# Attention scores of a gated linear attention layer with exchanged operands: four column groups, a copy by ScalarE and a turn by TensorE

## The chip, the core and the metric

The kernel runs on one core of one Trainium2 chip, as one launch. The metric is the device time of the launch in microseconds (us). Before the change it is 1719.86 us, the median of 3 runs (1718.37 to 1725.63).

## The reference

A decoder trunk of two layers for a prompt (1024 tokens) and 8 short samples (8 tokens each), in f32. Layer 0 mixes tokens by causal pooling, layer 1 by gated linear attention (GLA) with four heads. Only the prompt's part of layer 1 is touched by the change. Cut to it, for each head, with chunks of 32 tokens (`b` is the running sum of the log decay within a chunk):

```
q_dec = q * exp(bcum);  k_intra = k * exp(-bcum);  k_state = k * exp(blast - bcum)
att = where(causal, q_dec @ k_intra.T, 0)
o = att @ v + q_dec @ s                      # s: the state before the chunk
s = exp(blast) * s + k_state.T @ v
```

Then `o` is normed, gated by silu(z) and projected. The products are f32.

## The kernel before

Everything is written in Bass with explicit semaphores: each engine has its own list of instructions, and waits stand where the author put them. Nothing is reordered by a scheduler. TensorE is called PE in the rows, VectorE DVE, ScalarE ACT, GpSimd POOL.

The prompt is worked in 8 super-chunks of 128 tokens (`SUP = 4 * CH`, `NSUP = 8`), four chunks of 32 in each. With a decay that is summed over all 128 tokens, `Kp[:, b, :]` holds the 128 keys as chunk `b` of the queries sees them, and `qd` the 128 queries. In each head a loop over steps `s = 0..9` runs on three engines at once:

- **PE** (lines 1865 to 1887): `fill(1)`, then `scores(s+1)` (L1756, into the PSUM bank X[0]), `key_rows(s+1)` (L1766, a transpose by identity), `output(s)` (L1774: scores times values; L1782: queries times state, from s = 1), `update(s)` (L1791: the state's update, into ps[1][:, 2]), `fill(FILL_STEP - 1)`, which is one more fill, `mean_square` (L1846), on even steps from 2 `sample_inter` (L1811: the samples' queries times their state, in column groups of 32), and from step 2 `sample_update` (L1823, L1824), which overwrites ps[1][:, 2] and so waits for `S_ready` of the same step. A `fill` is one eighth of a gate projection Z0, Z1 or Z2: nine passes on L515 into psA. It has nothing to do with the recurrence and is put between its parts. Eight fills make a projection; the next one may start only when ACT has read psA out (`gate_in`, L1140, a Silu).
- **ACT** (lines 1148 to 1165): in step s `gate_in` if s is 0 or 4, `ksT_out(s+1)` (L1117), `exps(s+2)` (L1098 four times into Kp, L1102, L1105), `o_out(s)` (L1129, L1130), `exp_qs(s+1)` (L1111). Silu and Exp need different tables of ACT, so each `gate_in` has an ACT_TABLE_LOAD before it and the next `exps` has one too.
- **DVE** (lines 1472 to 1485): `ks_rows(s-2)`, `att_out(s+1)` (L1398: copies the scores under the causal mask to SBUF), `qd_args(s+2)` (L1376, L1377), `scale_qk(s+2)` (L1385, L1387), `state(s)` (L1406, L1410), `scale_qs(s+1)` (L1391), `sample_state(s-2)` (L1424).
- **POOL** multiplies Kp by the keys (L881) after each `exps`, then sums squares (L890, L892).

A semaphore count is per super-chunk: `att_done` is raised by `scores`, `att_ready` by `att_out`, `kp_ready` by POOL, `evac` by `gate_in`. `wait_apart` is a wait against a register's value.

Of the kernel before, what the change touches and what calls it, by code (L numbers as in the profile page):

```python
# [24 lines left out]
P = 128  # L25
# [5 lines left out]
KG = GW // P  # L31
# [10 lines left out]
CH = 32  # L42
SUP = 4 * CH
NSUP = TP // SUP
# [46 lines left out]
def trunk(nc, x_prompt, x_sample, c_prompt, c_sample, state_pool, state_gla, ada_w, ada_b, norm_g,  # L91
# [4 lines left out]
    ACT, ALU = mybir.ActivationFunctionType, mybir.AluOpType  # L96
# [3 lines left out]
    with ctx:  # L100
# [128 lines left out]
        def sem(name):  # L229
            return ctx.enter_context(nc.semaphore(name))  # L230
# [43 lines left out]
        kp_zero, kp_exp, kp_ready = sem("kp_zero"), sem("kp_exp"), sem("kp_ready")  # L274
        qd_arg, qd_exp, qd_ready = sem("qd_arg"), sem("qd_exp"), sem("qd_ready")
        qs_exp, qs_ready, ks_exp, ks_ready = sem("qs_exp"), sem("qs_ready"), sem("ks_exp"), sem("ks_ready")
        att_done, att_ready, o_done, o_evac = sem("att_done"), sem("att_ready"), sem("o_done"), sem("o_evac")
        kT_done, ksT_ready, upd_done, S_ready = sem("kT_done"), sem("ksT_ready"), sem("upd_done"), sem("S_ready")
        smp_arg, smp_exp, smp_ready = sem("smp_arg"), sem("smp_exp"), sem("smp_ready")
# [24 lines left out]
        def wait_apart(eng, what, count):  # L304


            count = eng.to_reg(count)
            eng.wait_ge(vec_ready, 1)
            eng.wait_ge(what, count)
# [606 lines left out]
        def _(act):  # L916
# [125 lines left out]
            def head(g, first):  # L1042
# [65 lines left out]
                def exp_qs(s):  # L1108
                    if s >= 1:
                        act.wait_ge(o_done, g * NSUP + s)  # L1110
                    nc.scalar.activation(qs[:], L[:, s * SUP:(s + 1) * SUP], ACT.Exp).then_inc(qs_exp, 1)  # L1111

                def ksT_out(s):
                    act.wait_ge(kT_done, g * NSUP + s + 1)
                    if s >= 2:
                        act.wait_ge(upd_done, g * NSUP + s - 1)
                    nc.scalar.activation(ksT[:, s % 2, :], ps[1][:, 1, 0:P], ACT.Copy).then_inc(ksT_ready, 1)  # L1117
# [31 lines left out]
                exp_qs(0)  # L1149
                act.wait_ge(smp_kT, g + 1)  # L1150
                nc.scalar.activation(ksT_s[:], ps[1][:, 1, 0:P], ACT.Copy).then_inc(smp_ksT, 1)
                ksT_out(0)
                exps(1)
                for s in range(NSUP):
                    if s in (0, 4):
                        gate_in(s // 4)
                    if s + 1 < NSUP:
                        ksT_out(s + 1)
                    if s + 2 < NSUP:
                        exps(s + 2)  # L1160
                    o_out(s)
                    if s + 1 < NSUP:
                        exp_qs(s + 1)
                    if s in (1, 5):
                        split_slot(L1, GP, act, g, GP.slot["Z2"] + s // 4)
# [44 lines left out]
        def _(dve):  # L1210
# [134 lines left out]
            with dve.Fori(0, NG) as g:  # L1345
# [25 lines left out]
                def qd_args(s):  # L1371

                    c0 = s * SUP
                    if s >= 1:
                        dve.wait_ge(att_done, g * NSUP + s)
                    nc.vector.tensor_copy(qd[:, 0:CH], L[:, c0:c0 + CH])  # L1376
                    nc.vector.tensor_tensor(qd[:, CH:SUP].rearrange("p (b t) -> p b t", b=3),  # L1377
                                            L[:, c0 + CH:c0 + SUP].rearrange("p (b t) -> p b t", b=3),
                                            L[:, c0 + CH - 1:c0 + SUP - 1:CH].unsqueeze(2).broadcast_to([P, 3, CH]),
                                            ALU.subtract).then_inc(qd_arg, 1)  # L1380
# [11 lines left out]

                def att_out(s):

                    if s >= 2:
                        wait_apart(dve, o_done, g * NSUP + s - 1)
                    wait_apart(dve, att_done, g * NSUP + s + 1)
                    nc.vector.copy_predicated(att[:, s % 2, :], causal[:], X[0][:, 0:P])\  # L1398
                        .then_inc(att_ready, 1)

                def state(s):
# [11 lines left out]
                def ks_rows(b):  # L1413

                    if b >= 1:
                        dve.wait_ge(smp_upd, g * NB + b)
                    link(nc.vector.tensor_scalar(ksm[:, 0, :], ksT_s[:], seq_rows[:, b:b + 1], None, ALU.mult))
                    nc.vector.scalar_tensor_tensor(out=ksm[:, 1, :], in0=ksT_s[:], scalar=seq_rows[:, b:b + 1],  # L1418
                                                   in1=ksm[:, 0, :].bitcast(f32), op0=ALU.mult,
                                                   op1=ALU.subtract).then_inc(ksm_ready, 1)  # L1420
# [51 lines left out]
                for s in range(NSUP + 2):  # L1472
                    if s >= 2:
                        ks_rows(s - 2)
                    if s + 1 < NSUP:
                        att_out(s + 1)
                    if s + 2 < NSUP:
                        qd_args(s + 2)
                        scale_qk(s + 2)
                    if s < NSUP:  # L1480
                        state(s)
                    if s + 1 < NSUP:
                        scale_qs(s + 1)
                    if s >= 2:
                        sample_state(s - 2)
# [43 lines left out]
        def _(pe):  # L1529
# [179 lines left out]
            def head(g, first):  # L1709
# [38 lines left out]
                def scores(s):  # L1748
                    pe.wait_ge(kp_ready, g * NSUP + s + 1)
                    pe.wait_ge(qd_ready, g * NSUP + s + 1)  # L1750
                    if s >= 1:
                        pe.wait_ge(att_ready, g * NSUP + s)
                    else:
                        pe.wait_ge(smp_attr, g + 1)
                    for b in range(4):
                        last = nc.tensor.matmul(X[0][:, b * CH:(b + 1) * CH], Kp[:, b, :], qd[:, b * CH:(b + 1) * CH],  # L1756
                                                start=True, stop=True)
                    last.then_inc(att_done, 1)

                def key_rows(s):  # L1760
                    pe.wait_ge(ks_ready, g * NSUP + s + 1)
                    if s >= 1:
                        pe.wait_ge(ksT_ready, g * NSUP + s)
                    else:
                        pe.wait_ge(smp_ksT, g + 1)
                    nc.tensor.transpose(ps[1][:, 1, 0:P], ks[:], ident[:]).then_inc(kT_done, 1)  # L1766

                def output(s):

                    pe.wait_ge(att_ready, g * NSUP + s + 1)  # L1770
                    if s >= 1:
                        pe.wait_ge(o_evac, g * NSUP + s)
                    for e in range(KG):
                        last = nc.tensor.matmul(ps[1][:, 0, e * P:(e + 1) * P], v[:, s, e * P:(e + 1) * P],  # L1774
                                                att[:, s % 2, :], start=(e == 0), stop=(s == 0 and e == KG - 1),
                                                skip_group_check=True)
                    if s:
                        pe.wait_ge(S_ready, g * NSUP + s)
                    pe.wait_ge(qs_ready, g * NSUP + s + 1)
                    if s:  # L1780
                        for e in range(KG):
                            last = nc.tensor.matmul(ps[1][:, 0, e * P:(e + 1) * P], S[:, e * P:(e + 1) * P],  # L1782
                                                    qs[:], start=False, stop=(e == KG - 1), skip_group_check=True)
                    last.then_inc(o_done, 1)

                def update(s):

                    pe.wait_ge(ksT_ready, g * NSUP + s + 1)
                    if s >= 3:
                        pe.wait_ge(s0_ready, g * NB + s - 2)  # L1790
                    nc.tensor.matmul(ps[1][:, 2, :], ksT[:, s % 2, :], v[:, s, :], start=True,  # L1791
                                     stop=True).then_inc(upd_done, 1)
# [72 lines left out]
                fill(1)  # L1865
                scores(0)
                key_rows(0)
                fill(FILL_START - 5)
                for s in range(NSUP + 2):
                    if s <= NSUP:  # L1870
                        fill(1)
                    if s + 1 < NSUP:
                        scores(s + 1)
                        key_rows(s + 1)
                    if s < NSUP:
                        output(s)
                        update(s)
                        fill(FILL_STEP - 1)
                    if 1 <= s <= NSUP:
                        pe.wait_ge(att_ready, g * NSUP + min(s + 2, NSUP))  # L1880
                        mean_square(s - 1)
                    if s in (2, 4, 6, 8):
                        sample_inter(s - 2)
                    if s == NSUP + 1:
                        sample_out()
                    if s >= 2:
                        sample_update(s - 2)
# [64 lines left out]
```

## Time and profile before

| what | value |
|---|---|
| median of 3 runs | 1719.86 us |
| the profiled execution | 1722.27 us |
| its span (first to last instruction) | 1720.5 us |
| granted TensorE clock, mean | 0.98 |
| PE busy / PEld (weight loads) busy | 96% / 91% |
| DVE, ACT, POOL busy | 48%, 28%, 23% |

The attention loops of the four heads start their first scores at about 895, 1117, 1340 and 1563 us of the span. Within a head the starts of the eight blocks of scores on L1756 lie 5.4, 5.7, 6.8, 8.3, 7.3, 8.3 and 7.3 us apart, the same in all four heads within 0.02 us.

Busy shares are averages over the whole span. In the steps of the attention PE is busy nearly without a gap, so the question for each edit is what PE has to do, and what it would have to wait for.

### The profile page before, as it was taken

What the parts mean: (1) busy time and instruction counts of PE and PEld (TensorE: products, weight loads), DVE (VectorE), ACT (ScalarE), POOL (GpSimd) and SP (SyncE); (2) the same over time, 40 slices, a digit from 0 to 9 for tenths busy, and PEclk for the clock granted to TensorE, in tenths of its full rate; (3) what the DMA queues carried; (4) which work ended last, traced back from release to release, by engine and by line L of the source; (5) the groups of instructions that cost most, each with busy time, mean ns of one, the idle gap of its engine ahead of it and who ended that gap; (6) DMA issues with size and microseconds to landing.
All of it is one profiled execution on the core that took longest, in us unless ns stands there. A gap on an engine that the chain in (4) does not pass through costs nothing.

```text
span 1720.5 us, 26408 instructions
## 1 busy us (share of the span) xinstructions
PE 1644.9 (96%) x10307; PEld 1564.1 (91%) x10307; DVE 833.3 (48%) x1245; ACT 483.5 (28%) x1021; POOL 397.3 (23%) x392
## 2 busy tenths in 40 slices
PE   6899999999999999997999999999999999999997
PEld 3798999999999999996898899988999889998896
DVE  4494439453844475456224561235621456324465
ACT  4321112110211111134335403264132532225423
POOL 3221212121221212113224121232112331213310
PEclk8999999999999999997999999999999999999999
DMA  9322211221222122210112211122111221111212
GB/s 352 129 62 72 75 44 55 74 76 39 67 76 62 53 66 71 67 27 26 37 38 75 80 39 50 37 62 80 51 38 37 62 92 38 41 47 38 98 43 104
DMA packets 145621, 115.23 MB, mean 67 GB/s; under 512 B 5885, under 2 KB 128345, under 8 KB 145506
## 3 DMA queue, kind: packets, MB, share of 16 engines
q1 hardware_dynamic: 143680, 112.87, 21.3%
q8 instruction: 91, 1.49, 0.4%
q10 hardware_dynamic: 1834, 0.74, 0.2%
q14 instruction: 16, 0.13, 0.0%
HBM read 99.05 MB, written 15.00 MB: 66 GB/s over the span
## 4 chain that ended last, share of the span: by engine, by line
PE 88%; DVE 8%; ACT 2%; issue 1%; DMA 1%; SPq 0%; POOL 0%; ACTq 0%; DVEq 0%
PE psA L515 45%; PE psB L515 29%; PE psB L1774 2%; PE psB L1791 2%; PE psX L1756 2%; DVE PQ L1273 2%; PE psB L1782 1%; PE psX L1811 1%; DMA ada<-in_ada_w 1%; PE psB L1823 1%; DVE y_rows L1523 1%; PE psX L1636 1%; DVE a_hi L591 1%; ACT PQ L1049 1%; DVE ksm L1418 1%
## 5 line engine op out<-in xcount | busy, mean ns | idle before, releaser
L322 POOL TENSOR_TENSOR w_lo<-stage,w_hi 128x1024 fp32r<-128x1024 f32 x112 | 279.0, 2492 | 1059.4 <-ACT w_hi L317 1059.4
L515 PE MATMUL psA<-h_hi,w_hi 128*128 128x362 f32 (+1 forms) x1152 | 277.4, 350 | 24.5 <-DVE h_lo L453 15.3
L515 PE MATMUL psA<-h_lo,w_hi 128*128 128x362 f32 (+1 forms) x1152 | 256.9, 332 | 0.0
L515 PE MATMUL psA<-h_hi,w_lo 128*128 128x362 f32 (+1 forms) x1152 | 255.6, 330 | 0.0
L515 PEld LDWEIGHTS psA<-h_hi,w_hi 128*128 128x128 f32 x1152 | 202.4, 192 | 53.5 <-issue 48.3
L317 ACT ACTIVATE w_hi<-stage 128x1024 fp32r<-128x1024 f32 x112 | 120.1, 1072 | 392.3 <-PE psB L515 301.3
L515 PEld LDWEIGHTS psA<-h_lo,w_hi 128*128 128x128 f32 x1152 | 204.2, 193 | 0.0
L515 PEld LDWEIGHTS psA<-h_hi,w_lo 128*128 128x128 f32 x1152 | 203.4, 192 | 0.0
L515 PE MATMUL psB<-h_hi,w_hi 128*128 128x362 f32 (+1 forms) x576 | 129.1, 332 | 1.7 <-ACT kT L1049 1.7
L515 PE MATMUL psB<-h_hi,w_lo 128*128 128x362 f32 (+1 forms) x576 | 126.3, 327 | 0.0
L515 PE MATMUL psB<-h_lo,w_hi 128*128 128x362 f32 (+1 forms) x576 | 126.2, 327 | 0.0
L515 PE MATMUL psA<-a_hi,w_hi 128*128 128x362 f32 (+1 forms) x480 | 108.2, 333 | 5.9 <-DVE a_lo L594 5.9
L515 PE MATMUL psB<-a_hi,w_hi 128*128 128x362 f32 (+1 forms) x480 | 106.0, 329 | 4.2 <-DVE a_lo L1294 4.2
L515 PE MATMUL psA<-a_lo,w_hi 128*128 128x362 f32 (+1 forms) x480 | 105.7, 328 | 0.0
L515 PE MATMUL psB<-a_hi,w_lo 128*128 128x362 f32 (+1 forms) x480 | 105.6, 328 | 0.0
L515 PE MATMUL psA<-a_hi,w_lo 128*128 128x362 f32 (+1 forms) x480 | 105.3, 327 | 0.0
L515 PE MATMUL psB<-a_lo,w_hi 128*128 128x362 f32 (+1 forms) x480 | 105.3, 327 | 0.0
L515 PEld LDWEIGHTS psB<-h_hi,w_hi 128*128 128x128 f32 x576 | 98.3, 189 | 7.4 <-issue 6.3
L1273 DVE SCALAR_TENSOR_TENSOR PQ<-PQ,win_on 128x1220 f32<-128x1220 f32 (+2 forms) x48 | 103.2, 2150 | 2.8 <-DVE PQ L1268 0.5
L515 PEld LDWEIGHTS psB<-h_hi,w_lo 128*128 128x128 f32 x576 | 99.9, 188 | 0.0
L515 PEld LDWEIGHTS psB<-h_lo,w_hi 128*128 128x128 f32 x576 | 99.8, 188 | 0.0
L1364 DVE COPY v<-psB 128x512 f32<-128x512 f32 x32 | 20.6, 686 | 150.2 <-PE psB L1719 150.2
(314 smaller groups left out, 2369.7 us busy)
## 6 DMA issues: line engine op xcount, KB each, us to landing
stage<-in_gla_w_in SPq DMA_DIRECT2D x40, 512.0 KB, 3.9
stage<-in_pool_w_in SPq DMA_DIRECT2D x32, 512.0 KB, 4.1
ada_stage<-in_ada_w SPq DMA_DIRECT2D x24, 512.0 KB, 3.5
ada<-in_ada_w SPq DMA_DIRECT2D x8, 1024.0 KB, 12.2
stage<-in_pool_w_out SPq DMA_DIRECT2D x16, 512.0 KB, 3.5
v<-in_state_gla SPq DMA_DIRECT2D x32, 256.0 KB, 2.6
out_new_gla_sample<-v SPq DMA_DIRECT2D x32, 256.0 KB, 2.1
stage<-in_gla_w_out SPq DMA_DIRECT2D x16, 512.0 KB, 3.6
```

Of the source, the lines that this page charges most:

```text
L317: nc.scalar.activation(w_hi[:, j % 2, :], stage[:, j % 2, :], ACT.Copy).then_inc(lay.hi_done, 1)
L322: nc.gpsimd.tensor_tensor(w_lo[:, j % 2, :], stage[:, j % 2, :], w_hi[:, j % 2, :].bitcast(f32), ALU.subtract).then_inc(lay.lo_done, 1)
L515: last = nc.tensor.matmul(ps[u][:, t, 0:width], weight(w[:, p, :], k), a[:, k, n0:n0 + width], start=(k == 0 and pas == 0), stop=(k == kt ...
L591: nc.vector.tensor_copy(a_hi[:, i, :], oT[:, i, :]).then_inc(chain_v, 1)
L1049: last = nc.scalar.activation(dst[:, n0:n0 + w], ps[GP.set[u]][:, t, 0:w], ACT.Copy, scale=scale)
L1273: link(nc.vector.scalar_tensor_tensor(out=dst[:, lo:WE], in0=src[:, lo - sh:WE - sh], scalar=win_on[:].rearrange("p g k -> p (g k)")[:, ds ...
L1364: nc.vector.tensor_copy(v[:, 4 * half:4 * half + 4, i * P:(i + 1) * P], ps[1][:, half, :].rearrange("p (s n) -> p s n", s=4))
L1418: nc.vector.scalar_tensor_tensor(out=ksm[:, 1, :], in0=ksT_s[:], scalar=seq_rows[:, b:b + 1], in1=ksm[:, 0, :].bitcast(f32), op0=ALU.mult, ...
L1523: nc.vector.scalar_tensor_tensor(out=y_rows[0:n, s, :], in0=ps_y[s % 3][0:n].rearrange("p a n -> p (a n)"), scalar=y_rms[0:n, s:s + 1], in ...
L1756: last = nc.tensor.matmul(X[0][:, b * CH:(b + 1) * CH], Kp[:, b, :], qd[:, b * CH:(b + 1) * CH], start=True, stop=True)
L1774: last = nc.tensor.matmul(ps[1][:, 0, e * P:(e + 1) * P], v[:, s, e * P:(e + 1) * P], att[:, s % 2, :], start=(e == 0), stop=(s == 0 and e ...
L1791: nc.tensor.matmul(ps[1][:, 2, :], ksT[:, s % 2, :], v[:, s, :], start=True, stop=True).then_inc(upd_done, 1)
```

## The change

`scores` exchanges its operands. Before, a chunk's 128x128 keys were the weights and its 32 queries moved past them, one chunk after the other, and the result stood as keys by queries. Now a chunk's 32 queries are the weights, in one of four column groups of 32, and its 128 keys move; the four results stand in four groups of partitions, as queries by keys. `output` needs keys by queries. So ACT copies the block from PSUM to SBUF (`scores_out`, into the second half of `att`), and PE turns it by identity (`turn_scores`) into the same place of PSUM from where DVE masks it. `att` has one buffer for the masked scores now in place of two. The rest is the order: `turn_scores(s+1)` stands behind `update(s)`, `scores_out(s+1)` first in ACT's step, and `qd_args` ahead of `att_out` on DVE.

```diff
+                def scores_out(s):
+                    act.wait_ge(att_done, g * NSUP + s + 1)
+                    if s >= 1:
+                        act.wait_ge(turn_done, g * NSUP + s)
+                    nc.scalar.activation(att[:, 1, :], X[0][:, 0:P], ACT.Copy).then_inc(score_out, 1)
...
                 exp_qs(0)
                 act.wait_ge(smp_kT, g + 1)
                 nc.scalar.activation(ksT_s[:], ps[1][:, 1, 0:P], ACT.Copy).then_inc(smp_ksT, 1)
+                scores_out(0)
                 ksT_out(0)
                 exps(1)
                 for s in range(NSUP):
+                    if s + 1 < NSUP:
+                        scores_out(s + 1)
                     if s in (0, 4):
                         gate_in(s // 4)
...
                 def att_out(s):
-                    if s >= 2:
-                        wait_apart(dve, o_done, g * NSUP + s - 1)
-                    wait_apart(dve, att_done, g * NSUP + s + 1)
-                    nc.vector.copy_predicated(att[:, s % 2, :], causal[:], X[0][:, 0:P])\
+                    if s >= 1:
+                        wait_apart(dve, o_done, g * NSUP + s)
+                    wait_apart(dve, turn_done, g * NSUP + s + 1)
+                    nc.vector.copy_predicated(att[:, 0, :], causal[:], X[0][:, 0:P])\
                         .then_inc(att_ready, 1)
...
+                    if s + 2 < NSUP:
+                        qd_args(s + 2)
                     if s + 1 < NSUP:
                         att_out(s + 1)
                     if s + 2 < NSUP:
-                        qd_args(s + 2)
                         scale_qk(s + 2)
...
-                        last = nc.tensor.matmul(X[0][:, b * CH:(b + 1) * CH], Kp[:, b, :], qd[:, b * CH:(b + 1) * CH],
+                        last = nc.tensor.matmul(X[0][b * CH:(b + 1) * CH, 0:P], qd[:, b * CH:(b + 1) * CH], Kp[:, b, :],
                                                 start=True, stop=True)
                     last.then_inc(att_done, 1)
+
+                def turn_scores(s):
+                    pe.wait_ge(score_out, g * NSUP + s + 1)
+                    nc.tensor.transpose(X[0][:, 0:P], att[:, 1, :], ident[:]).then_inc(turn_done, 1)
...
-                                                att[:, s % 2, :], start=(e == 0), stop=(s == 0 and e == KG - 1),
+                                                att[:, 0, :], start=(e == 0), stop=(s == 0 and e == KG - 1),
...
                 scores(0)
                 key_rows(0)
+                turn_scores(0)
                 fill(FILL_START - 5)
...
                     if s < NSUP:
                         output(s)
                         update(s)
+                    if s + 1 < NSUP:
+                        turn_scores(s + 1)
+                    if s < NSUP:
                         fill(FILL_STEP - 1)
```

ACT, from the end of `exps(1)` into step 0 of the first head, before (PQ<-psA is `gate_in`, ksT<-psB is `ksT_out`, Kp<-L is `exps`):

```order
L1102 ACTIVATE qd<-qd 128x128 [waits qd_arg]
L1105 ACTIVATE ks<-L 128x128 [waits kT_done]
L1140 ACT_TABLE_LOAD
L1140 ACTIVATE PQ<-psA 128x364 [waits gla_unit_done]
L1140 ACTIVATE PQ<-psA 128x362 x2
L1117 ACTIVATE ksT<-psB 128x128 [waits kT_done]
L1098 ACT_TABLE_LOAD
L1098 ACTIVATE Kp<-L 128x32 [waits att_done]
```

The same place after the change (all lines of ACT's part have moved by some numbers; att<-psX is `scores_out`):

```order
L1103 ACTIVATE qd<-qd 128x128 [waits qd_arg]
L1106 ACTIVATE ks<-L 128x128 [waits kT_done]
L1119 ACTIVATE att<-psX 128x128 [waits turn_done,att_done]
L1148 ACT_TABLE_LOAD
L1148 ACTIVATE PQ<-psA 128x364 [waits gla_unit_done]
L1148 ACTIVATE PQ<-psA 128x362 x2
L1125 ACTIVATE ksT<-psB 128x128 [waits kT_done]
L1099 ACT_TABLE_LOAD
L1099 ACTIVATE Kp<-L 128x32 [waits att_done]
```

The copy of the scores, with its wait for `att_done`, now stands between the last exponential and the load of the Silu table, which had no wait ahead of it.

DVE, in step 0 of the first head, before (att<-causal,psX is `att_out`, the writes of qd and ks are `scale_qk`, S<-psB is `state`):

```order
L1398 COPY_PREDICATED att<-causal,psX 128x128 [waits att_done,vec_ready]
L1376 COPY qd<-L 128x32 [waits att_done]
L1377 TENSOR_TENSOR qd<-L 128x96
L1384 REGISTER_ALU
L1385 TENSOR_TENSOR qd<-qd,qT 128x128 [waits qd_exp]
L1387 TENSOR_TENSOR ks<-ks,kT 128x128 [waits ks_exp]
L1404 ISA
L1406 COPY S<-psB 128x512 [waits upd_done,S_stored]
```

And after:

```order
L1388 TENSOR_TENSOR qd<-L 128x96
L1409 COPY_PREDICATED att<-causal,psX 128x128 [waits vec_ready,turn_done,o_done]
L1395 REGISTER_ALU
L1396 TENSOR_TENSOR qd<-qd,qT 128x128 [waits qd_exp]
L1398 TENSOR_TENSOR ks<-ks,kT 128x128 [waits ks_exp]
L1415 ISA
L1417 COPY S<-psB 128x512 [waits upd_done,S_stored]
```

`att_out` has moved behind the arguments of qd, and waits for the turn and for the output before it; both scalings and the state's update stand behind it.

## Rows read from the trace of the kernel before

**Rows 1.** The page: busy time and the chain that ended last.

```profile
PE 1644.9 (96%) x10307; PEld 1564.1 (91%) x10307; DVE 833.3 (48%) x1245; ACT 483.5 (28%) x1021; POOL 397.3 (23%) x392
...
PE 88%; DVE 8%; ACT 2%; issue 1%; DMA 1%; SPq 0%; POOL 0%; ACTq 0%; DVEq 0%
```

**Rows 2.** The chain in step 5 of head 0: start us, length us, what.

```profile
937.27 0.81 PE psX L1756 x8
938.08 0.14 PE psB L1766
938.22 0.89 PE psB L1774 x8
939.11 0.89 PE psB L1782 x8
940.01 0.86 PE psB L1791 x2
940.87 1.50 PE psA L515 x9
```

**Rows 3.** The chain around a product in column groups of layer 0.

```profile
155.80 0.57 PE psX L1636 x16
156.38 1.71 PE psB L515 x9
```

**Rows 4.** Timeline, head 0, before and in steps 0 and 1: start us, length us, what.

```profile
896.36 0.28 ACT L1117 ACTIVATE ksT<-psB 128x128 f32<-128x128 f32 x1 [2.36 <-PE psB L1766]
...
900.65 0.97 PE L1756 MATMUL psX<-qd,Kp 128*128 128x32 f32 x8
900.85 1.20 ACT L1140 ACTIVATE PQ<-psA 128x364 f32<-128x364 f32 x3 [1.50 <-PE psA L515]
...
903.53 1.03 ACT L1098 ACTIVATE Kp<-L 128x32 f32<-128x32 f32 x4
...
904.64 1.45 POOL L881 TENSOR_TENSOR Kp<-Kp,kT 128x32 f32<-128x32 f32 x4 [5.57 <-ACT Kp L1098]
...
906.33 0.97 PE L1756 MATMUL psX<-qd,Kp 128*128 128x32 f32 x8
```

**Rows 5.** Timeline, head 0, end of step 3 and step 4.

```profile
925.72 1.28 ACT L1140 ACT_TABLE_LOAD   x1
...
928.76 0.97 PE L1756 MATMUL psX<-qd,Kp 128*128 128x32 f32 x8
928.96 1.20 ACT L1140 ACTIVATE PQ<-psA 128x364 f32<-128x364 f32 x3 [1.96 <-PE psA L515]
...
932.90 0.29 DVE L1385 TENSOR_TENSOR qd<-qd,qT 128x128 f32<-128x128 f32 x1 [2.49 <-ACT qd L1102]
...
933.44 0.74 DVE L1410 SCALAR_TENSOR_TENSOR S<-S,dec,psB 128x512 f32<-128x512 f32 x1
...
935.04 0.19 PEld L1823 LDWEIGHTS psB<-v_s,ksm 128*128 128x128 f32 x1 [0.84 <-issue]
```

**Rows 6.** Timeline, head 0, step 5.

```profile
938.21 0.30 DVE L1398 COPY_PREDICATED att<-causal,psX 128x128 f32<-128x128 int8 x1 [1.07 <-PE psX L1756]
...
939.67 0.29 DVE L1385 TENSOR_TENSOR qd<-qd,qT 128x128 f32<-128x128 f32 x1 [0.92 <-ACT qd L1102]
...
939.97 0.33 DVE L1387 TENSOR_TENSOR ks<-ks,kT 128x128 f32<-128x128 f32 x1
...
940.91 0.75 DVE L1410 SCALAR_TENSOR_TENSOR S<-S,dec,psB 128x512 f32<-128x512 f32 x1 [0.61 <-PE psB L1791]
...
942.31 0.19 PEld L1823 LDWEIGHTS psB<-v_s,ksm 128*128 128x128 f32 x1
```

**Rows 7.** Busy us (instructions) of PE, PEld, DVE, ACT, POOL; granted clock; DMA.

```profile
960.70:964.10 3.40, 2.00 (x18) 1.81 (x16) 3.06 (x3) 2.54 (x5) 2.13 (x1) 1.00 0.29 106
964.13:967.54 3.41, 3.02 (x9) 2.83 (x10) 1.68 (x3) 0.56 (x1) 0.96 (x3) 0.50 0.01 5
...
199.50:202.90 3.40, 1.96 (x12) 1.96 (x13) 1.52 (x4) 0.00 (x0) 0.00 (x0) 1.00 0.45 154
```

More of the change, by code:

```diff
@@ L276, in trunk @@
         qs_exp, qs_ready, ks_exp, ks_ready = sem("qs_exp"), sem("qs_ready"), sem("ks_exp"), sem("ks_ready")
+        score_out, turn_done = sem("score_out"), sem("turn_done")
         att_done, att_ready, o_done, o_evac = sem("att_done"), sem("att_ready"), sem("o_done"), sem("o_evac")
```

## The prediction

> **What bounds the kernel now.** I read the page first. PE is busy for 96% of the span and makes up 88% of the chain that ended last [rows 1], so a change counts by what it adds to PE's own work or by what PE has to wait for. The granted clock is 0.98 on average. Next the chain inside one step of the attention [rows 2]: PE runs without a hole, and the step is a plain sum. The scores take 0.81 us for 8 passes (each f32 product is two), the transpose of the keys 0.14, the two halves of the output 0.89 each, the update 0.86, one fill of nine passes 1.50. Last the timeline of ACT, DVE and POOL beside it, to see how early each product of theirs is: the places where a delay would show are the two steps of a head with a Silu (steps 0 and 4), where ACT has no slack. There the Silu starts 0.20 us after the first scores, at 900.85 against 900.65 and at 928.96 against 928.76 [rows 4, 5], since it reads what PE's last fill has just left, and its table was loaded long before, at 925.72, while ACT waited [rows 5].
>
> **PE's own work.** The scores are 32 blocks (8 steps, 4 heads). No row shows a block of 4 products in column groups with 128 moving columns, but layer 0 has one with 8 products, 16 passes [rows 3]. It stands in the chain with 0.57 us, and the nine passes behind it take 1.71 where they take 1.50 elsewhere [rows 2, 3]: 0.21 us go into changing over. Passes of four groups run beside each other: a round of four takes about a quarter of the time of four in a row. Half of the 16 passes cost 0.22 less (two rounds of about 0.11), so our block costs 0.57 - 0.22 + 0.21 = 0.56 us, against 0.81. That is -0.25 a block. Bounds: at best the whole of 16 passes is halved, 0.28 + 0.21 = 0.49; at worst the eight passes run one after the other at the 0.11 of today's, plus the changeover, 1.1 us, so -0.32 to +0.3. I take -0.25, since the row is of the same form. The turn is one pass of the form of the keys' transpose, +0.14 [rows 2]. Both together are -0.1 us a step, -3.2 us in 32 blocks, if nothing waits.
>
> The Trainium skill (TensorEngine Tiling (Array Packing), "Theoretical Speedup") gives up to four times for a dimension of 32 or less. By that the blocks would go from 0.81 to 0.20 us, an estimate of -19.5 us in all, and -15 with the turns. The Trainium skill (TensorEngine Tiling (Array Packing), "Key Properties") also says that changing the tiling mode drains the engine, and the trace agrees with that one: 0.21 us behind such a block [rows 3]. By the drain most of the fourfold is given back.
>
> **The first block of a head.** Nothing but the keys' transpose stands between `scores(0)` and `turn_scores(0)`. ACT needs 0.28 us for its copy [rows 4] and about 0.15 for the two hand-overs. The scores have landed about 0.52 after their start (the 0.56, less what the changeover takes behind them), so the turn can't begin before 0.52 + 0.05 + 0.28 + 0.20 = 1.05 us and ends its pass at 1.19; before, the fill behind began at 0.81 + 0.14 = 0.95. So +0.24 us a head, where the cover of the other steps (output and update) is missing.
>
> **Step 0: the copy ahead of the Silu.** `scores_out(1)` waits for `att_done`, and it stands ahead of the table load in ACT's order. Until now the load was hidden in ACT's idle time. Now it follows: scores done at 900.65 + 0.52 = 901.17; hand-over 0.05, copy 0.28, a little to retire, load 1.28 [rows 4, 5], so the Silu starts at 902.82, not 900.85: ACT is 1.97 us late with everything queued behind it in the step. Who waits for that?
> - PE's next fill needs psA, which the Silu frees at 902.82 + 1.20 = 904.02. PE is there at 900.65 + 0.56 + 0.14 + 0.89 + 0.86 + 0.14 = 903.24 (step 0 has only one half of the output). It starts about 904.13: a wait of 0.9.
> - The next scores need Kp. Its exponentials move from 903.53 to 905.50, POOL's product from 904.64 to 906.61, ending at 908.06 in place of 906.09 [rows 4]. PE, after two fills, is there at 904.13 + 3.00 = 907.13: another 0.9.
> The second block of scores then starts at 908.05 and not at 906.33 [rows 4]: +1.72 us a head.
>
> **Step 4.** The same shift: scores done at 929.28, Silu at 930.94, not 928.96, +1.98. psA is free at 932.14, when PE just arrives (two halves of the output), and Kp is early. But on DVE the update of the state stands behind the scaling of qd and ks, which needs ACT's exponentials: qd moves from 932.90 to 934.88, the state from 933.44 to 935.42, ending at 936.16 [rows 5]. `sample_update` may not overwrite the update before that; its weights, loaded at 935.04 now, would be due at 934.94 and go in at about 936.2. +1.25, less 0.1 for PE's own work: +1.15 us a head.
>
> **Steps 3 and 5.** Here `sample_update` comes soon, there is no `sample_inter` before it. `att_out` now waits for the turn and takes scaling and state with it. With the scores started at 937.11, the turn begins 0.56 + 0.14 + 0.89 + 0.89 + 0.86 = 3.34 later, at 940.45, and lands about 0.3 later (its pass is short, its latency not); 0.13 hand-over, then copy 0.30, qd 0.29, ks 0.33, which overlap a little, and the state 0.75 [rows 6]: done about 942.45, against 941.66 now. The weights on L1823 would be due at 942.31 - 0.10 = 942.21 [rows 6]. A wait of 0.25 to 0.35, net +0.2 in each of the two. In steps 2 and 6 `sample_inter` covers it, in step 1 there is no such product: -0.1 each. The single `att` buffer costs nothing: the turn stands behind `o_done` of the output anyway, and the scores of the next step come a fill later. `qd_args` ahead of `att_out` keeps ACT's exponential of qd from waiting for the turn.
>
> Sum of a head: 0.24 + 1.72 + 1.15 + 2 x 0.2 - 3 x 0.1 = 3.2 us, 12.8 us in four heads.
>
> **The clock.** At the end of the first head PE is idle for 1.40 us between narrow products (busy 2.00 of 3.40), and then the granted clock is 0.50 for 3.41 us [rows 7], 1.2 GHz in place of 2.4, which costs half of that, 1.7 us. A stretch in layer 0 with as little (1.96 of 3.40), but with wide passes around it, is followed by full clock [rows 7]. The change adds two holes of 0.9 in steps 0 and 1 and one of 1.25 in step 4, this one behind the narrow `sample_inter`. None to all eight could bring such a drop, 0 to 13.6 us. I take two, +3.4: the hole of step 4 is the kind that did it, yet shorter.
>
> So the profiled execution would go from 1722.3 by 12.8 + 3.4 = 16 to about 1738; against the median of the runs, which is 2.4 below that execution, 1736 us.
>
> **Rivals.**
> - *No late Silu.* If ACT's Silu came in time in spite of the order (the table load running while ACT waits for `att_done`), the copy would cost it only 0.33 + 0.32 us, both waits of step 0 and the one of step 4 would shrink to nearly nothing, and the sum is the -3.2 of PE's work plus 1 to 3: 1717 to 1720, no change. For it: loads do stand ahead of waits today (925.72). Against it: after the change the load has the waiting copy ahead of it on an engine that works in order. It decides from the point where ACT's delay falls under about 0.8 us. 0.11.
> - *Faster.* The same, and the column groups give the fourfold with little changeover: -10 to -15, 1705 to 1711. Against it is the 0.21 of [rows 3]. 0.05.
> - *The column groups do not run beside each other* with 128 moving columns, +0.5 a block over my term: 16 us more, 1752. Against it [rows 3]. 0.03.
> - *The clock falls in every hole*: eight drops, 12.8 + 13.6: 1746. 0.17.
> - *The forecast*, with zero to four drops, 1731 to 1741. 0.64.
>
> The range holds the forecast, most of the clock's rival, and reaches towards the first: 1725 to 1748. About 0.5% (8.6 us) is what a measurement of this kernel can tell from no change: faster 0.05 (the fourfold), within it 0.13 (the first rival and a tail of 0.02 of the forecast), slower 0.82 (the rest).
>
> **What would show it.** In the profile after: blocks of scores with about 0.35 us in the chain and 1.7 for what follows; PE's waits named by ACT's Silu (psA) and POOL's Kp in step 0, by DVE's state ahead of `sample_update` in steps 3, 4, 5; the Silu 2.2 us behind the scores and not 0.2; starts of the scores 7.4 apart in step 0 in place of 5.7, and 9.5 in place of 8.3 in step 4. I am wrong if the load stands ahead of the copy in time, or if the head is not some 3 us longer.

## The result: 6.4 us slower, where 15 were forecast

| | before | after |
|---|---|---|
| median | 1720.79 us (16 runs, 1717.23 to 1725.63) | 1727.21 us (16 runs, 1723.78 to 1731.89) |
| ratio after / before | | 1.0043, 95% interval 1.0035 to 1.0051 |
| the profiled execution / its span | 1722.27 / 1720.5 us | 1723.78 / 1722.1 us |
| mean granted clock of that execution | 0.98 | 0.983 |

The changed kernel is slower beyond its interval, in the direction of the forecast, but the 1727.2 us lie far below the 1736 that were named, and the move is less than half of the one forecast. The two medians differ by 6.4 us. The ratio is not that of the two medians: 1.0043 of 1720.8 us is 7.4 us, its interval 6.0 to 8.8 us.

The profiled execution of the changed kernel happens to be the fastest of its 16. Its first scores of the first head start at 892.25 us, 3.0 us earlier than the 895.21 of before, though nothing is changed ahead of them. So the two traces are compared step by step and not by their spans.

The page after the change, lines of [rows 1]:

```profile
PE 1635.3 (95%) x10339; PEld 1535.2 (89%) x10339; DVE 842.3 (49%) x1245; ACT 491.5 (29%) x1053; POOL 397.4 (23%) x392
...
PE 59%; issue 24%; DVE 8%; POOL 5%; ACT 3%; DMA 1%; SPq 0%; POOLq 0%; ACTq 0%; DVEq 0%
```

PE is busy for 10 us less (the 32 more passes are the turns), and the kernel takes longer all the same: PE waits. Up to some 2.6 us of the 10 are not less work but a higher mean clock in this execution (0.983 against 0.980 of 1720 us is 5 us less at half speed). The waits of PE from 885 us on, engine, line and whom it waited for, total us, times, longest:

```profile
PE psB L1840 <- DVE ksm L1429: 7.3, 4, 1.8
PE psB L1840 <- DVE S L1421: 4.8, 4, 1.3
...
PE psA L516 <- ACT PQ L1148: 3.4, 4, 0.9
...
PE psX L1768 <- POOL Kp L882: 2.9, 4, 0.8
```

The first was there before the change (it is the hole at the heads' ends of [rows 7]). The other three are new, one of each in a head: 1.2 for the state in step 4, 0.9 for psA and 0.7 for Kp in step 0 and 1. These are the three large waits that the prediction named; its smaller ones, behind the first block and in steps 3 and 5, are no rows of this list. Step 0 in the timeline after the change (start, length, what; it answers to [rows 4]):

```profile
897.80 0.43 PE L1768 MATMUL psX<-Kp,qd 128*32 128x128 f32 x8
...
898.29 0.28 ACT L1119 ACTIVATE att<-psX 128x128 f32<-128x128 f32 x1 [3.60 <-PE psX L1768]
...
898.59 1.28 ACT L1148 ACT_TABLE_LOAD   x1
...
899.88 1.20 ACT L1148 ACTIVATE PQ<-psA 128x364 f32<-128x364 f32 x3
...
901.14 0.77 PE L516 MATMUL psA<-h_hi,w_hi 128*128 128x364 f32 x3 [0.79 <-ACT PQ L1148]
...
903.67 1.44 POOL L882 TENSOR_TENSOR Kp<-Kp,kT 128x32 f32<-128x32 f32 x4 [7.94 <-ACT Kp L1099]
...
905.16 0.43 PE L1768 MATMUL psX<-Kp,qd 128*32 128x128 f32 x8 [0.77 <-POOL Kp L882]
```

ACT sat idle for 3.6 us in front of the copy, and only then loads the table. The Silu starts 2.08 us behind the scores (0.20 before).

The chain in step 5 of the first head, which answers to [rows 2]:

```profile
936.74 0.35 PE psX L1768 x8
937.10 0.26 PE psB L1783
937.35 0.89 PE psB L1791 x8
...
940.00 0.11 PE psX L1775
940.11 1.49 PE psA L516 x9
941.60 0.12 PE psX L1863 x2
941.72 0.03 issue
941.74 0.47 PE psB L1840
```

Block and transpose take 0.61 us, where 0.95 stood; the turn adds 0.11.

Starts of the eight blocks of scores, as distances (us, first head; the others agree within 0.05), and from the last block to the last update of the state:

| | first | step 0 | 1 | 2 | 3 | 4 | 5 | 6 and 7 | sum |
|---|---|---|---|---|---|---|---|---|---|
| before | 5.44 | 5.68 | 6.80 | 8.34 | 7.28 | 8.35 | 7.28 | 10.13 | 59.30 |
| forecast, difference | +0.24 | +1.72 | -0.1 | -0.1 | +0.2 | +1.15 | +0.2 | -0.1 | +3.2 |
| after, difference | +0.11 | +1.68 | -0.22 | -0.23 | -0.03 | +1.23 | -0.07 | -0.32 | +2.13 |

Over the four heads that is 8.6 us. The runs differ by 6.4 by their medians and by 7.4 by the ratio. So two things are to be explained: why a head lost 2.1 and not 3.2 us, and whether another 1 to 2 us were given back somewhere. The second is small: the ratio's interval still holds the 8.6.

### The profile page after: what moved, and what is told of

Read it like the earlier page. It is cut to its first block, busy times and chain, and to the rows that moved or that the text cites. A ratio compares the mean times of both kernels' runs of the same rounds, so it can differ in the third digit from the quotient of the medians.

```text
span 1722.1 us, 26536 instructions
## 1 busy us (share of the span) xinstructions
PE 1635.3 (95%) x10339; PEld 1535.2 (89%) x10339; DVE 842.3 (49%) x1245; ACT 491.5 (29%) x1053; POOL 397.4 (23%) x392
## 4 chain that ended last, share of the span: by engine, by line
PE 59%; issue 24%; DVE 8%; POOL 5%; ACT 3%; DMA 1%; SPq 0%; POOLq 0%; ACTq 0%; DVEq 0%
PE psA L516 28%; PE psB L516 21%; POOL w_lo L323 4%; DVE PQ L1284 2%; PE psB L1799 1%; PE psB L1791 1%; PE psB L1808 1%; POOL Kp L882 1%; DMA ada<-in_ada_w 1%; PE psB L1840 1%; DVE y_rows L1535 1%; PE psX L1648 1%; DVE a_hi L592 1%; PE psX L1828 1%; PE psX L1768 1%
## 5 line engine op out<-in xcount | busy, mean ns | idle before, releaser
L516 PE MATMUL psA<-h_hi,w_hi 128*128 128x362 f32 (+1 forms) x1152 | 266.5, 340 | 27.3 <-DVE h_lo L454 15.9
L516 PEld LDWEIGHTS psA<-h_hi,w_hi 128*128 128x128 f32 x1152 | 198.6, 191 | 52.6 <-issue 46.3
```

What stands on the lines that cost most here:

```text
L516: last = nc.tensor.matmul(ps[u][:, t, 0:width], weight(w[:, p, :], k), a[:, k, n0:n0 + width], start=(k == 0 and pas == 0), stop=(k == kt ...
```

## The experiments

### after_again: the changed kernel once more

No edit.

> The changed kernel as it is. My sum had 3.2 us a head from waits and PE's own work and 3.4 us in all from the granted clock. Theory A (the heads are 2.1 us longer, as the starts and ends of their steps in the trace after say, 8.5 us in four heads, and the clock gives some 2 us back): 6 to 7 us over the kernel before, with the mean granted clock of the runs at or above that of before. Theory B (the trace after was taken in an execution with few clock drops, and the clock takes nothing back on average): 8 to 9 us over before, mean clock the same or lower.

Measured: 1727.73 us (5 runs) against 1720.58 (12 runs of before on the same chip), ratio 1.0043 (1.0030 to 1.0055). The mean granted clock over all executions of the changed kernel (21) is 0.9806, over those of the kernel before (41, in the three jobs) 0.9790. A difference of 0.0016 is some 5 us less at half speed, up to 2.7 us of time. That is theory A's sign; the 7.1 us here (interval 5.2 to 9.5) lie between the two theories, and the two kernels' clocks alone don't say why.

### silu_first: the order on ACT

```diff
                 for s in range(NSUP):
-                    if s + 1 < NSUP:
-                        scores_out(s + 1)
                     if s in (0, 4):
                         gate_in(s // 4)
+                    if s + 1 < NSUP:
+                        scores_out(s + 1)
```

> The changed kernel, but in steps 0 and 4 the Silu (gate_in) stands ahead of the copy of the scores on ACT, so its table load again has no wait ahead of it. If the late Silu is the whole loss (step 0 7.36 us in place of 5.68, step 4 9.58 in place of 8.35), ACT is only 0.23 us later than before: step 0 about 5.66, step 4 about 8.1, the other steps as in the changed kernel (0.2 us shorter than before where PE is not waiting). A head is then about 1.0 us shorter than before: 1716 to 1717, 4 us under the kernel before. The rival (the copy, the turn and the column groups cost this by themselves, wherever the copy stands) expects no gain over the changed kernel: 1727.

Measured: 1715.15 us (6 runs), ratio to before 0.9968 (0.9956 to 0.9979). Step 0 took 5.57 us, step 4 8.11, all others as in the changed kernel; a head 58.16 in place of 61.43. Two statements in another order are worth 12 us. ACT in step 0:

```profile
895.90 1.28 ACT L1148 ACT_TABLE_LOAD   x1
...
898.99 0.43 PE L1768 MATMUL psX<-Kp,qd 128*32 128x128 f32 x8
899.10 1.20 ACT L1148 ACTIVATE PQ<-psA 128x364 f32<-128x364 f32 x3 [1.91 <-PE psA L516]
...
900.17 0.30 ACT L1119 ACTIVATE att<-psX 128x128 f32<-128x128 f32 x1
```

The load is back in ACT's idle time and the copy costs 0.3 us behind the Silu. No wait of PE for psA, Kp or the state is left. The prediction had this as its first rival, with -3.2 us of PE's work: as a mechanism it was right, it only was not what the changed kernel does.

### copy_alone: the other half, on the kernel before

```diff
+                def scores_copy(s):
+                    act.wait_ge(att_done, g * NSUP + s + 1)
+                    nc.scalar.activation(SZ[:, 0:P], L[:, 0:P], ACT.Copy)
...
                 for s in range(NSUP):
+                    if s + 1 < NSUP:
+                        scores_copy(s + 1)
                     if s in (0, 4):
                         gate_in(s // 4)
```

> The kernel before, with one thing added: ACT waits for att_done and copies 128x128 values (from SBUF to SBUF, its result is used by nobody) at the start of each of the steps 0 to 6, ahead of the Silu and its table load. If the order on ACT is what costs, the Silu comes 2.4 us later than before (the scores end 0.45 us later here than in the changed kernel): step 0 7.85 us in place of 5.68, step 4 9.9 in place of 8.35, other steps unchanged; 3.8 us a head, about 15 us in all: 1735. The rival (copy and wait are hidden, the loss is in PE's new operations) expects 1720 to 1721.

Measured: 1732.07 us (4 runs), ratio 1.0069 (1.0055 to 1.0084). Step 0 7.90 us, step 4 10.02, 0.05 and 0.12 over the expectation, step 1 0.1 longer than before. A head is 4.0 us longer, 16 in all, but the runs differ by 11.5 (interval 9.5 to 14.5). With no new product and no new layout, the wait ahead of the table load costs more than the whole change. The gap between the steps' sum and the runs, 4.5 us, is wider than in the changed kernel and beyond the interval; the mean clock of its 4 executions is 0.983 against 0.979, 7 us less at half speed, up to 3.6 us of time.

### groups_alone: the price of the block

```diff
-                scores_out(0)
                 ksT_out(0)
...
-                    if s + 1 < NSUP:
-                        scores_out(s + 1)
...
-                    wait_apart(dve, turn_done, g * NSUP + s + 1)
+                    wait_apart(dve, att_done, g * NSUP + s + 1)
...
-                turn_scores(0)
...
-                    if s + 1 < NSUP:
-                        turn_scores(s + 1)
```

> The changed kernel without the copy by ACT and without the turn: DVE masks the scores as they come out of the column groups. It leaves out the turn, so the scores that it uses are turned wrongly. It prices the block in column groups: by my term, a block costs 0.56 us where it cost 0.81, 8 x 0.25 = 2.0 us a head, 8 us in all: 1713. By the chain of the trace after (0.35 for the block and 0.12 more on the transpose behind it, 0.47 in all) it is 0.34 a block: 2.7 a head, 11 us in all: 1710. If the column groups had their full fourfold it would be 0.6 a block, 19 us: 1701.

Measured: 1707.50 us (6 runs), ratio 0.9934 (0.9920 to 0.9948). This kernel leaves out the copy by ACT as well as the turn. Every step is 0.28 to 0.36 us shorter than before, the stretch from the last block on 0.43, 2.8 a head, 11 in all (the runs' interval is 8.9 to 13.8). The chain in step 5:

```profile
933.48 0.35 PE psX L1765 x8
933.84 0.26 PE psB L1780
934.10 0.89 PE psB L1788 x8
```

So a block saves 0.34 us, not the 0.25 of my sum, and not the 0.6 of a fourfold. The 0.35 of the block itself is what the prediction had (0.57 - 0.22); what follows it takes 0.12 more than before (0.26 for 0.14), not 0.21. The copy and the turn, which the kernel needs, take back 1.6 us of the 2.8 a head even in silu_first.

### keys_first: what the changeover depends on

In silu_first, `key_rows(s + 1)` stands ahead of `scores(s + 1)` on PE, from step 0 on.

```diff
-                        scores(s + 1)
                         key_rows(s + 1)
+                        scores(s + 1)
```

> The silu_first kernel with the transpose of the keys ahead of the scores in PE's step, so that f32 products of full width (the output) follow the column groups and not a transpose. In silu_first block and transpose take 0.36 + 0.26 us, 0.12 of it changeover by the transpose's own 0.14. If the changeover is the same behind any block (theory A), the two take 0.61 again and the steps stay, 1715. If a full-width product pays the 0.21 that the layer-0 rows show (theory B), each step is 0.1 us longer, 2.5 to 3 us in all, 1718; that would tell why my term of 0.56 was too high.

Measured: 1716.25 us (10 runs), ratio 0.9972 (0.9962 to 0.9982): 1.1 us over silu_first. The intervals of the two ratios overlap, so the steps decide: a head is 0.3 us longer. The chain:

```profile
935.49 0.11 PE psB L1783
935.60 0.35 PE psX L1768 x8
935.95 1.09 PE psB L1791 x8
```

The eight passes of the output behind the block take 1.09 us, 0.20 more than their 0.89: the changeover of [rows 3]. The transpose takes 0.11. Behind the block the transpose takes 0.26, 0.15 more. So theory B holds for the changeover, but not in full for the steps: steps 1 to 5 are 0.05 to 0.07 us longer, the first interval 0.11, step 0 and the last stretch 0.05 shorter. My term put the full 0.21 behind a transpose, where 0.12 to 0.15 was due. What of PE's work the extra time is, no run takes apart.

### turn_covered: the first turn, and the mask in steps 3 and 5

On silu_first:

```diff
-                turn_scores(0)
-                fill(FILL_START - 5)
+                fill(1)
+                turn_scores(0)
+                fill(FILL_START - 6)
...
-                    if s + 1 < NSUP:
+                    late = s in (3, 5)
+                    if s + 1 < NSUP and not late:
                         att_out(s + 1)
                     if s + 2 < NSUP:
                         scale_qk(s + 2)
                     if s < NSUP:
                         state(s)
+                    if late:
+                        att_out(s + 1)
```

> The silu_first kernel with two moves: the first turn of a head stands one fill later, and in steps 3 and 5 DVE masks the scores after the state's update, not before. It prices two of my terms. If the first block of scores costs its uncovered copy (0.24 in my sum), the first interval shrinks from 5.55 to 5.2 or 5.3. If steps 3 and 5 lose 0.15 to 0.25 us each to the state behind the mask, they shrink from 7.27 and 7.21 to 7.05, the value of a step without waits. Together 0.6 to 0.8 us a head: 1712 to 1713. The rival (no such waits, the copy and turn simply take this PE time) expects no interval to change, 1715.

Measured: 1713.04 us (5 runs), ratio 0.9947 (0.9934 to 0.9961), 2.1 us under silu_first; the intervals of the two ratios overlap, so the steps decide. First interval 5.21 in place of 5.55, steps 3 and 5 both 7.04 in place of 7.25 and 7.21, step 0 0.05 longer; 0.65 to 0.7 us a head, 2.7 in all. The 7.04 are the 6.94 of groups_alone with the turn's 0.11, so nothing else of the new order costs time there, the single `att` buffer included. The waits that the prediction put there are real, 0.34 behind the first block and 0.2 in steps 3 and 5. They were hidden in the after column of the table by a larger saving of PE's own.

### squares_first: the hole at the heads' ends

On silu_first, in POOL's list:

```diff
-                    if s == NSUP:
-                        lo_slots(L1, GP, pool, g, GP.slot["O01"])
                     square_sum(s)
+                    if s == NSUP:
+                        lo_slots(L1, GP, pool, g, GP.slot["O01"])
```

> The silu_first kernel, and on POOL the split of the weights O01 (2.3 us) stands behind the sum of squares of the samples and not ahead of it. At the end of each head PE waits 1.82 us for ksm on DVE, whose last step takes 2.49 us beside that split and 0.35 elsewhere. Theory (the hole is the split's, and the granted clock falls behind this hole and behind none of the holes that the change made): the 1.8 us go in each head, 7.3 us; and the clock's half-speed stretches behind the heads' ends (5 of 3.4 us in the trace of silu_first) go too, up to 1.7 us each: 1700 to 1708 for 1715.2. Rival (the clock's drops have nothing to do with the hole): 7.3 us and no more, 1708, with drops at the heads' ends as before.

Measured: 1702.41 us (4 runs), ratio 0.9889 (0.9874 to 0.9904), 12.7 us under silu_first. In silu_first, the split on POOL and DVE's subtraction run side by side:

```profile
959.06 2.34 POOL L323 TENSOR_TENSOR w_lo<-stage,w_hi 128x1024 fp32r<-128x1024 f32 x1 [5.31 <-ACT w_hi L318]
959.08 2.47 DVE L1429 SCALAR_TENSOR_TENSOR ksm<-ksT_s,seq_rows,ksm 128x128 fp32r<-128x128 f32 x1
...
961.61 0.79 PE L1840 MATMUL psB<-v_s,ksm 128*128 128x512 f32 x1 [1.82 <-DVE ksm L1429]
```

With the split behind:

```profile
959.35 0.35 DVE L1429 SCALAR_TENSOR_TENSOR ksm<-ksT_s,seq_rows,ksm 128x128 fp32r<-128x128 f32 x1
...
959.87 0.47 PE L1840 MATMUL psB<-v_s,ksm 128*128 128x512 f32 x1
...
961.38 2.40 POOL L323 TENSOR_TENSOR w_lo<-stage,w_hi 128x1024 fp32r<-128x1024 f32 x1
```

DVE's subtraction (L1429) has two inputs in SBUF and lasts until 0.15 us behind the end of POOL's instruction, which reads SBUF and had started 0.02 us before it; without that neighbour it takes 0.35 us. The Trainium skill, page SBUF — State Buffer, section Who interferes with whom, says that a VectorE instruction with two SBUF inputs contends with a GpSimd instruction that reads SBUF, that the ports they share are an exclusive lock, and that the order of issue decides who blocks. By that rule the move takes 2.1 us off DVE's instruction, and the trace agrees.

The same stretch in the two, silu_first in the first fence and squares_first in the second (us, then busy us and instructions of PE, PEld, DVE, ACT, POOL, the granted clock, DMA):

```profile
960.93:967.75 6.82, 6.14 (x19) 5.95 (x20) 3.98 (x4) 0.86 (x1) 1.26 (x3) 0.50 0.35 115
```

and squares_first:

```profile
960.93:967.75 6.82, 6.82 (x42) 6.58 (x42) 6.37 (x8) 3.78 (x5) 2.77 (x3) 1.00 0.33 116
```

PE does 42 passes in it and not 19 (the first 0.7 us of the 6.82 are still the hole in silu_first). 7.3 us of the gain are the four holes, and the other 5.4, by subtraction, the clock: the trace of squares_first has no stretch at half speed in the attention, silu_first had five of 3.4 us. The distances between the heads' first scores agree. Behind the third head, where silu_first had no such stretch, the gain is 1.9 us, the hole alone; behind the first and second, where it had two each, it is 4.8 and 4.4. In the attention of these traces TensorE fell from 2.4 to 1.2 GHz only behind this hole; there are other stretches at half speed ahead of the attention and behind it, in all traces.

### before_squares and after_squares: the 2 us

The POOL move of squares_first, once on the kernel before and once on the changed one.

> The kernel before with the POOL move of squares_first alone. Its heads' ends lose the hole of 1.82 us, 7.3 us in all, and the drops of the clock behind them, 5 stretches in the trace of before, 1.7 us each at most: 1705 to 1710. If the drops were not the hole's, 1713.

> The changed kernel with the same POOL move: the holes of 0.8, 0.8 and 1.2 us that the change made stay, the hole of 1.82 us at the heads' ends goes. Theory A (the two kernels have all their differences in the steps of the attention, 8.6 us by the trace, and 2 us of these were given back because the clock fell more rarely behind the heads' ends of the changed kernel): without the hole nothing is given back, after_squares is 8 to 9 us over before_squares, both with the same mean clock and no drop in the attention. Theory B (the clock gives back wherever the changed kernel has a hole, or the difference lies elsewhere): 6 to 7 us over before_squares, as after over before. Theory C (my prediction's clock term: the new holes do bring drops): 10 us or more, with drops behind steps 0 and 4.

Measured: before_squares 1706.72 us (5 runs), ratio to before 0.9934 (0.9920 to 0.9948); after_squares 1715.21 us (11 runs), 0.9977 (0.9966 to 0.9988). By the medians the change costs 8.5 us without the hole at the heads' ends, what the steps say (8.6), and 6.4 to 7.1 with it. By the ratios it is 0.0043 in both cases, 7.4 us, with some 3 us to either side without the hole. So the runs' times do not tell theory A from theory B.

The traces say more. In before_squares and after_squares no stretch of the attention is at half speed, and from one head's first scores to the next head's the change costs 2.24, 2.28 and 2.34 us: some 9 us in four heads. In the traces of before and after, the same three distances grow by 0.84, 0.30 and 1.23 us; there before had 1, 1 and 2 stretches at half speed behind the old hole, and after 0, 0 and 1. That is where this pair of traces differs by less than its steps. The trace of after_squares, over all steps of the first head with its three new holes (PE busy 77.05 of 80 us):

```profile
895.00:975.00 80.00, 77.05 (x507) 64.66 (x506) 40.43 (x80) 42.67 (x102) 26.39 (x47) 1.00 0.23 77
```

The granted clock is 1.00 throughout, and so in the other heads: theory C, my clock term, falls. Whether the clock really falls less often behind the old hole in the changed kernel stays open. Its two traces have 2 and 3 such stretches and before has 5, but other kernels with the same hole have 1 (copy_alone), 2 (groups_alone), 4 (keys_first), 5 (silu_first) and 7 (turn_covered), so one trace of each kernel can't decide it. For it speak the mean clocks over all executions, 0.9806 against 0.9790.

### both_moves: the fastest version

squares_first and turn_covered together.

> The silu_first kernel with the moves of squares_first and of turn_covered. They touch different places, so the gains should add: 7 to 15 us for the one and 2.5 for the other, 1698 to 1706, the fastest of all kernels here. If it is slower than squares_first, the moves disturb each other.

Measured: 1698.16 us (4 runs), ratio to before 0.9861 (0.9845 to 0.9876). It is 4.2 us under squares_first, more than the 2.9 that its steps account for (57.44 us a head in place of 58.15); with 4 runs each the rest is within the spread from run to run. It beats both kernels. Most of its gain is not the change's: before_squares alone is 12.4 us under the kernel before. The other 8.6 to before_squares are what the change is worth with the Silu first and its small waits covered.

## Why the prediction was off

By its own steps, with the measured number beside each:

- **Step 0, the copy ahead of the Silu: right.** +1.72 a head forecast, +1.68 measured, with the waits at 0.9 and 0.9 forecast, 0.8 to 0.9 and 0.7 to 0.8 measured. copy_alone and silu_first show it from both sides. A slip of 0.06 us in it: the scores were put at 908.05, while the product they wait for ends at 908.06 and needs a hand-over (in the trace it ends at 905.11, and the scores start at 905.16).
- **Step 4: right.** +1.15 forecast, +1.23 measured, through the state on DVE as said. There is some luck in how close it came: the late Silu costs the step 1.47 us (9.58 against 8.11 in silu_first) where 1.25 stood, and PE's own saving is 0.23 and not 0.1.
- **PE's own work: mis-sized, the sign right.** The step that failed is the one that took 0.25 us for a block. A block saves 0.34 (groups_alone). Its own 0.35 came true; I put the changeover seen behind layer 0's block, 0.21 ahead of a full-width pass, on top of a transpose, where it is 0.12 (groups_alone) to 0.15 (keys_first), and the turn is 0.11 and not 0.14. Over 32 blocks this is 3.8 us too little saving. The sentence that most of the fourfold is given back by the drain doesn't hold either: of the 0.27 us that are missing to it, 0.12 stand behind the block and 0.15 in the block itself (0.35 for 0.20).
- **First block, steps 3 and 5: the waits about right, the sum hidden.** 0.34 us behind the first block, where the +0.24 contained a wait of 0.35 (1.05 less 0.56 and 0.14), and 0.2 in steps 3 and 5, where 0.25 to 0.35 stood (turn_covered). The rest of their difference is PE's own saving again.
- **The clock: drops that did not come.** The other step that failed is "I take two, +3.4". None of the new holes brought a drop in any trace; they are twelve, three in a head, and not the eight that the prediction counted. The rows had offered two cases, a hole that did and one that did not, and I read the new holes as the first kind because narrow products stand around them. This is 3.4 us. Whether, beyond it, 1 to 2 us came back behind the old hole is not shown.
- The rival "no late Silu" fell for this kernel (its waits are there), "column groups not side by side" fell (a block has landed after 0.43 us), and so did "the clock falls in every hole". The fourfold fell with groups_alone.

The case without a drop rests on two neighbouring stretches of layer 0, of which [rows 7] has only the first. The second (same columns as there):

```profile
202.90:206.30 3.40, 3.40 (x22) 3.40 (x21) 1.64 (x5) 0.00 (x0) 0.00 (x0) 1.00 0.00 0
```

The sum: forecast were 12.8 + 3.4 = 16.2 us (the 1736 are 16 over the 1719.9 known then, 15 over the 1720.8 of the 16 runs). The steps cost 8.6, which is 4.2 less, and the drops nothing, 3.4 less. Measured are 6.4 by the medians and 7.4 by the ratio; the 1.2 to 2.2 us between that and 8.6 are open, and the interval, up to 8.8, allows for none.

## What to carry to other kernels

- An instruction with a new wait should never stand ahead of something that the engine used to do in its idle time. Here a copy of 0.28 us, put ahead of a table load that had no wait, cost 12 us. One place later, steps 0 and 4 are only 0.17 and 0.10 us longer than without copy and turn (silu_first against groups_alone), and 0.11 of that is the turn.
- The price of a changeover between column groups and full width is paid by what follows. Take it from a row with the same follower, or keep both ends in the sum.
- A hole ahead of half-speed stretches can be dearer than the hole (5.4 us on top of 7.3 in squares_first, by subtraction). Count such stretches in several executions before a term for the clock goes into a sum: with the same hole, the traces here have one to seven of them.

## What the runs showed that I had not expected

- DVE's scalar_tensor_tensor on SBUF operands took 2.47 us beside POOL's 2.34 us tensor_tensor and 0.35 us without it; moving POOL's instruction behind other work gave 12.7 us.
- Holes of 0.7 to 1.26 us in PE brought no drop of the granted clock, twelve of twelve in each of the traces of the changed kernel and of after_squares.
- A block of eight passes with 32 weights' columns and 128 moving columns in four groups has landed 0.43 us after its start, with 0.35 in the chain, where eight passes of full width with 32 moving columns took 0.81.
